# A hybrid encoder on one core: V's turns one a step, projection loads reordered, the time transform's parts alternating, products of zeros ahead of a preparation

## The reference

```
def trunk(x, ...):
    h = rmsnorm(x, attn_norm)
    q, k, v, z = split(h @ attn_w_in, 4)          # 8 heads, two maps of 64 a head, v of 128
    s = q @ k.T * 64 ** -0.5 - slope[head] * abs(t - s)     # for each of the two maps
    p = softmax(s)
    o = (p[:, :, 0] - lam * p[:, :, 1]) @ v
    o = rmsnorm(o, subln_g) * (1 - lam_init)      # over a head's 128
    x = x + (o * silu(z)) @ attn_w_out
    h = rmsnorm(x, fnet_norm)
    u, z = split(h @ fnet_w_in, 2)
    f = real(fft2(u per group of 128, over time and channel))
    x = x + (f * silu(z)) @ fnet_w_out
    return rmsnorm(x, final_norm)
```

## Time and profile before

| | us |
|---|---|
| median of 3 runs | 3275.3 (3273.77 to 3275.41) |
| the profiled execution | 3275.25, span 3273.6 |
| TensorE busy | 2995.3, 91% of the span |
| VectorE, ScalarE, GpSimd busy | 1605.8, 1341.3, 788.7 |
| mean granted TensorE clock | 0.954 of full speed |

### The profile page before, as it was taken

The page is one execution under the profiler, slowest core; times in us unless marked ns, Lnnn a source line. Parts: engine busy times, 40 slices in busy tenths (PEclk is TensorE's granted clock), DMA queues, the critical chain, the costliest instruction groups (busy, mean ns, idle before and its releaser), DMA issues. The chain is left out here.

```text
span 3273.6 us, 42276 instructions
## 1 busy us (share of the span) xinstructions
PE 2995.3 (91%) x15084; PEld 2511.9 (77%) x15084; DVE 1605.8 (49%) x1832; ACT 1341.3 (41%) x2294; POOL 788.7 (24%) x392
## 2 busy tenths in 40 slices
PE   6999999999689999999999999995998898996599
PEld 4888888888568787878787878783677898975487
DVE  7323221111178787878787878784774101431222
ACT  6111100011167776667676767673342322221221
POOL 1223223223022222212121212123331320220552
PEclk9999999999899999999999999997999998898799
DMA  5333332222434313131313131104453513444653
GB/s 171 119 114 113 125 103 67 75 66 67 111 95 151 99 33 99 34 99 33 97 34 93 40 91 41 38 28 160 165 189 114 194 68 105 119 134 144 238 178 109
DMA packets 226332, 340.27 MB, mean 104 GB/s; under 512 B 22315, under 2 KB 172139, under 8 KB 220668
## 3 DMA queue, kind: packets, MB, share of 16 engines
q1 hardware_dynamic: 221548, 321.23, 31.1%
q0 software_dynamic: 4608, 16.78, 1.9%
HBM read 224.68 MB, written 126.03 MB: 107 GB/s over the span
## 5 line engine op out<-in xcount | busy, mean ns | idle before, releaser
L817 DVE TENSOR_REDUCE pa_half_max<-pa_score 128x1 f32<-128x1024 f32 x512 | 625.4, 1222 | 287.7 <-PE pa_score L630 287.7
L760 ACT ACTIVATE pa_p<-pa_score,pa_neg_max 128x1024 f32<-128x1024 f32 x512 | 567.2, 1111 | 74.4 <-DVE pa_neg_max L823 71.1
L894 POOL TENSOR_SCALAR pa_p<-pa_p,pa_inv_sum,pa_lam_neg 128x2048 f32<-128x2048 f32 x128 | 262.6, 2052 | 1072.9 <-DVE pa_inv_sum L844 1072.9
L687 PE MATMUL pa_o_acc<-pa_wt,pa_vv 128*128 128x256 f32 x2048 | 506.6, 381 | 0.1
L626 PE MATMUL pa_score<-pa_ka,pa_qa 128*128 128x512 f32 x1024 | 462.4, 452 | 39.9 <-DMA pa_kb<-const_position 27.0
L118 PE MATMUL ia_acc<-ia_xh,ia_wh 128*128 128x512 f32 (+1 forms) x1280 | 471.8, 369 | 0.0
L119 PE MATMUL ia_acc<-ia_xl,ia_wh 128*128 128x512 f32 (+1 forms) x1280 | 471.7, 368 | 0.0
L120 PE MATMUL ia_acc<-ia_xh,ia_wl 128*128 128x512 f32 (+1 forms) x1280 | 471.4, 368 | 0.0
L630 PE MATMUL pa_score<-pa_kb,pa_qb 96*128 96x512 f32 x1024 | 433.6, 423 | 0.0
L740 ACT ACTIVATE pa_wt<-pa_turned 128x512 f32<-128x512 f32 x512 | 306.0, 598 | 298.6 <-PE pa_turned L658 298.2
L687 PEld LDWEIGHTS pa_o_acc<-pa_wt,pa_vv 128*128 128x128 f32 x2048 | 371.4, 191 | 43.6 <-issue 0.3
(11 more groups left out here) (224 smaller groups left out, 4355.3 us busy)
## 6 DMA issues: line engine op xcount, KB each, us to landing
ia_raw<-attn_w_in POOLq DMA_DIRECT2D x32, 512.0 KB, 5.5
qk_hi<-ia_stage SPq DMA_DIRECT2D x64, 256.0 KB, 2.1
qk_lo<-ia_stage SPq DMA_DIRECT2D x64, 256.0 KB, 2.1
pa_ka<-qk_hi SPq DMA_DIRECT2D x32, 512.0 KB, 6.6
fl_slices<-normed SPq DMA_DIRECT2D x26, 512.0 KB, 6.6
pa_vt<-v SPq DMA_DIRECT2D x8, 1152.0 KB, 5.5
oa_b_in<-o SPq DMA_DIRECT2D x18, 512.0 KB, 4.8
oa_g_in<-attn_gate SPq DMA_DIRECT2D x18, 512.0 KB, 5.9
```

The costliest lines, as they stand in the source:

```text
L687: mm = pe.matmul(o_acc[:], vv[:, k], wt[:, g % 2, k], start=k == 0, stop=k == NB - 1)
L760: act.activation(dst[:, half * HALF:(half + 1) * HALF], score[:, (4 * q + j) % RING].rearrange("p a b -> p (a b)"), ACT.Exp, bias=neg_max[ ...
L817: dve.tensor_reduce(half_max[:, q % 2, n, half:half + 1], score[:, (4 * q + j) % RING].rearrange("p a b -> p (a b)"), AX_X, ALU.max).then_ ...
L894: pool.tensor_scalar(p1[:, par], p1[:, par], inv_sum[:, par, 1:2], lam["neg"][:, 0:1], ALU.mult, ALU.mult).then_inc(p1_scaled, 1)
```

## The change

Four places are changed.

1. In attention one V turn is made in each of the steps 1 to 5, between the third and the fourth quarter of the pair products; ScalarE copies it between its third and fourth exponential. The wait of the second half of a head's first pair for V's last blocks moves to step 5, and V's next load to step 6.
2. In the output projections branch and gate have semaphores of their own, and the row weight has one. Loads, ScalarE's, VectorE's and GpSimd's first operations are put into another order, and in the first projection PE's sums of squares 2 to 5 stand between the products of the first two row tiles.
3. In the Fourier layer the end sums of all even parts are made ahead of the even parts and copied to a tile, and the parts come as even 0, even 1, odd 0, even 2, odd 1, even 3, odd 2, odd 3, on PE and on ScalarE.
4. Ahead of the preparation PE makes 32 products of a tile of zeros, and it waits there only for the channel table; the other two constants are waited for before the time transform.

```diff
@@ attend
-            order += [(t, "v", c) for c in {1: (0, 1), 2: (2,), 3: (3, 4)}.get(t, ())]
+            order += [(t, "v", t - 1)] if 1 <= t <= NC + 1 else []
...
-                    if follows and q == 5:
-                        hold(sp, sp_held, turns, unit(h, 3, "v", 4) + 1)
+                    if follows and q == 6:
+                        hold(sp, sp_held, turns, unit(h, NC + 1, "v", NC) + 1)
                         load_v(h + 1)
...
-                        last = unit(h, 3, "v", NC - 1) if q == 4 else unit(h, q - 1, "w", NC - 1)
-                        pe.wait_ge(turned_out, last + 1)
+                        pe.wait_ge(turned_out, unit(h, q - 1, "w", NC - 1) + 1)
                         wait(pe, o_copied, OUTS * (h - back) + g)
+                    if k0 == 8 and q == 5:
+                        pe.wait_ge(turned_out, unit(h, NC, "v", NC - 1) + 1)
...
                     pair(2)
+                    turn_value(q - 1)
                     pair(3)
-                    for c in range(NC + 1):
-                        turn_value(c)
...
                     exp(2)
+                    if parts["score"] and (q, "v", q - 1) in place:
+                        take_v(h, q, q - 1)
                     exp(3)
-                    for c in range(NC + 1):
-                        if parts["score"] and (q, "v", c) in place:
-                            take_v(h, q, c)
@@ project_rows, SP
-                load_unit(0)
+                load_branch(0)
                 if rms:
-                    sp.dma_start(row_w[:], subln).then_inc(consts_in, 16)
-                load_weight(0)
-                load_weight(1)
-                load_unit(1)
-                if rms:
+                    sp.dma_start(row_w[:], subln).then_inc(row_in, 16)
+                    load_weight(0)
+                    load_branch(1)
+                    load_gate(0)
+                    load_weight(1)
+                    load_gate(1)
+                else:
+                    load_gate(0)
+                    load_weight(0)
+                    load_weight(1)
+                    load_unit(1)
+                for k in range(2, 4):
+                    load_weight(k)
+                if columns is not None:
                     sp.dma_start(ident[:], ident_dram).then_inc(consts_in, 16)
                     sp.dma_start(norm_w[:], column_norm).then_inc(consts_in, 16)
                 if final_norm is not None:
                     sp.dma_start(fn[:], final_norm.to_broadcast([P, D])).then_inc(consts_in, 16)
-                for k in range(2, KB):
+                load_unit(2)
+                for k in range(4, KB):
                     load_weight(k)
-                for n in range(2, 4):
-                    load_unit(n)
+                load_unit(3)
@@ project_rows, GpSimd
-                weight(1)
-                weight(3)
-                for n in range(N_UNITS):
...
-                    if n < 2:
-                        weight(2 * n + 5)
...
+                if rms:
+                    weight(1)
+                    gated_unit(0)
+                else:
+                    gated_unit(0)
+                    weight(1)
+                weight(3)
+                if rms:
+                    weight(5)
+                    gated_unit(1)
+                else:
+                    gated_unit(1)
+                    weight(5)
+                weight(7)
+                for n in range(2, N_UNITS):
+                    gated_unit(n)
@@ project_rows, PE
-                if columns is not None:
-                    pe.wait_ge(consts_in, 16 * n_consts)
...
+                        if rms and k % 2 == 1:
+                            sum_squares(k // 2 + 2)
...
-                    for n in range(3):
-                        sum_squares(n)
+                    sum_squares(0)
+                    sum_squares(1)
                 first_pair(0)
-                if rms:
-                    sum_squares(3)
                 first_pair(1)
-                if rms:
-                    sum_squares(4)
-                    sum_squares(5)
+                if columns is not None:
+                    pe.wait_ge(consts_in, 16 * n_consts)
@@ project_rows, ScalarE, second projection
-                    for k in range(4):
+                    weight(0)
+                    high(0)
+                    for k in range(1, 4):
                         weight(k)
-                    high(0)
+                    high(1)
                     for k in range(4, KB):
                         weight(k)
-                    high(1)
@@ project_rows, VectorE, first projection
                     weight(0)
-                    weight(2)
                     head_inverse(0, 0)
                     head_inverse(0, 1)
                     head_scale(0)
-                    weight(4)
+                    weight(2)
                     head_inverse(1, 0)
                     head_inverse(1, 1)
                     head_scale(1)
+                    weight(4)
                     weight(6)
@@ fourier_layer
+        time_order = [("even", 0), ("even", 1)]
+        for q in range(2, PAIRS):
+            time_order += [("odd", q - 2), ("even", q)]
+        time_order += [("odd", PAIRS - 2), ("odd", PAIRS - 1)]
+        units += [("nyquist",)] + time_order
...
-                pe.wait_ge(consts_in, 64)
...
+                pe.wait_ge(zeroed, 2)
+                for n in range(32):
+                    pe.matmul(ps[:, 7], ac[:, 0, 0, :P], ac[:, 0, 0, :GROUP], start=True, stop=True)
+                pe.wait_ge(consts_in, 32)
                 for g in range(N_PREP):
                     prepare(g)
...
+                pe.wait_ge(ends_in, 32)
...
                 even_transform(PAIRS)
                 for q in range(PAIRS):
-                    even_transform(q)
-                pe.wait_ge(tables_in, 128)
-                pe.wait_ge(out_lo, len(rows_units))
-                for q in range(PAIRS):
-                    odd_transform(q)
+                    mm = end_sum(q)
+                mm.then_inc(ends_summed, 1)
+                for kind, q in time_order:
+                    if (kind, q) == ("odd", 0):
+                        pe.wait_ge(tables_in, 128)
+                        pe.wait_ge(out_lo, len(rows_units))
+                    (even_transform if kind == "even" else odd_transform)(q)
...
+                for kind, q in time_order:
+                    (take_even if kind == "even" else turn_rows)(q)
```

More of the change, by code:

```diff
@@ L1835, in even_transform @@
                             pe.matmul(out[rows, 0], cos_cols(q, 1, 2 * TB)[0:1], extra[0:1], start=False, stop=True)
[L1836 to L1840 removed]
+                        else:
+                            mm = last
+                    if q == PAIRS:
+                        mm = end_sum(q)
                     mm.then_inc(products, 1)
```

89 lines of the change are left out of this document (55 added, 34 removed).

## The result

The changed kernel takes 3168.3 us (median of 4 runs, 3167.35 to 3170.64) where the kernel before takes 3274.6: a ratio of 0.9677, 95% interval 0.9666 to 0.9689, 106 us less. The forecast was 3162. The profiled execution has a span of 3165.3 us instead of 3273.6. Two executions lie far above all others, one of high_free (3419.9 us) and one of the kernel before (6791.5), and are left out of every comparison.

| stage | before | after | gain | forecast |
|---|---|---|---|---|
| attention | 1340.5 | 1283.4 | 57.1 | 57 |
| first output projection | 310.9 | 293.7 | 17.2 | 17 |
| gate projection | 211.7 | 212.0 | -0.2 | 0 |
| Fourier layer, to `nyquist` | 191.0 | 173.4 | 17.6 | 18 |
| Fourier layer, time transform | 89.4 | 82.9 | 6.5 | 9 |

A forecast was written before the change was run, and what follows sets the result against it. PE was busy 91% of the span, so outside its idle 278 us only its waits and low clock could be won. Gains 57 + 17 + 18 + 9 + 12 = 113 us from 3275.3 gave 3162; range 3150 to 3188.

The forecast's parts named there:

- V's turns: Attention: one V turn per step removes PE's waits for V's copies and the low clock behind; gain 57 us, bounds 39 to 64.
- The new wait in front of a V turn: Attention, steps 2, 4 and 5: the V turn after `pair(2)` waits 0.25 us for weight turn 3's copy.
- B: Attention: all 40 V turns wait 0.7 us for the third weight copy; gain only 39, time 3180; chance 0.10.
- C: Attention: V's copy is late for the next step's first turn; at 2.55 us wait plus 1.2 low clock each, 3309; chance 0.03.
- First output projection: Its start: earlier square, reciprocals and gating bring PE's first product 18.8 us earlier; gain 17 us, bounds 10 to 21.
- The first link: First output projection: row weight, with its own semaphore, lands 5.7 us after the stage's first load, letting ScalarE's first square start.
- Preparation: Fourier layer: 32 zeros raise the clock, so the preparation takes 22.4 us instead of 41.0; gain 18 us, bounds -6.4 to 20.
- rival A: Fourier layer: the preparation stays at or falls back to half clock; term +18 becomes about -4, time 3184; chance 0.15.
- Time transform: Fourier layer: odd part 0 two evens earlier brings the high halves' stores forward; gain 9 us, bounds 5 to 12.
- Second output projection: PE starts 18.3 us earlier, then waits 3.6 for GpSimd before the second pair; gain 12 us, bounds 8 to 16.
- The last three terms: Forecast gains of the Fourier layer's preparation, 18 us, its time transform, 9, and the second output projection, 12.
- the sum 113: Whole kernel: the five terms 57 + 17 + 18 + 9 + 12 add, since barriers close the stages; forecast 3162 us.

The follow-up runs named there:

- u_time: Changed kernel with the time transform's parts in the old order, evens then odds, end sums behind each even part: 3175.7 us, ratio 0.9701.
- u_oa: Changed kernel with the first output projection's old orders and waits for all constants, separate semaphores kept, no row-weight wait on ScalarE: 3184.0 us, ratio 0.9726.
- u_zero: Changed kernel without the 32 products of zeros and PE's wait for the zero tile: 3181.1 us, ratio 0.9716.

## The experiments: what the prediction had left uncertain

**Narrow zeros, and fewer** (zeros_narrow, zeros_16).

```diff
-                for n in range(32):
-                    pe.matmul(ps[:, 7], ac[:, 0, 0, :P], ac[:, 0, 0, :GROUP], start=True, stop=True)
+                for n in range(48):
+                    pe.matmul(ps[:, 7, :P + 2], ac[:, 0, 0, :P], ac[:, 0, 0, :P + 2], start=True, stop=True)
```
```diff
-                for n in range(32):
+                for n in range(16):
```

> The changed kernel with 48 products of zeros of 130 columns in place of 32 of 512; at the low clock 48 x 0.215 = 10.3 us, the same length as now. Theory (products as short as the preparation's own keep PE busy but do not raise the clock): the preparation starts where it does now and takes 41 us at 0.50; 18.9 lost and 1 to 2 more, 3168 + 20 = 3188. Rival 1 (it is the unbroken run of products, without the preparation's handovers between groups, that raises it): 22 us at 1.00, 3168. Rival 2 (the clock rises in the course of the preparation): 3175 to 3182.

> The changed kernel with 16 products of zeros in place of 32. In the changed kernel's trace the zeros go at half speed for the first 6 us and the first low part is there 5.5 us after they start. Theory (once the clock has risen nothing more is needed): 16 zeros take some 6.5 us, the preparation starts 3 to 3.6 us earlier and runs at 1.00; 3168 - 3 = 3165. Rival (the clock has not yet risen at their end, or falls at once in the first group): the preparation takes 41 us, 3168 - 3.5 + 20 = 3184.

Measured: narrow 3184.9 us, ratio 0.9728 (0.9712 to 0.9744), the Fourier layer 18.7 us longer; sixteen 3166.1 us, 0.9671 (0.9655 to 0.9687), that stage 3.7 us shorter. The windows of the stage's start and of the preparation, narrow zeros first, then sixteen:

```profile
2676.94:2688.43 11.49, 10.30 (x49) 10.30 (x49) 4.59 (x5) 3.17 (x3) 0.00 (x0) 0.51 0.78 273
2688.43:2729.47 41.04, 41.04 (x193) 40.97 (x193) 15.20 (x26) 13.73 (x27) 2.19 (x1) 0.50 0.26 81
```
```profile
2678.83:2686.30 7.47, 6.29 (x16) 4.97 (x17) 2.68 (x4) 2.12 (x2) 0.00 (x0) 0.55 0.81 283
2686.30:2708.62 22.32, 22.15 (x193) 21.66 (x191) 17.12 (x28) 14.81 (x28) 0.50 (x1) 1.00 0.65 195
```

The same 10 us of zeros, 130 columns wide, leave the clock at 0.50 through the zeros and all of the preparation, 51 us of nearly unbroken work. Behind 6.3 us of zeros 512 columns wide the preparation runs at 1.00 from start to end, PE busy for 22.15 of 22.32 us. With the width another thing changes: weight loads (PEld) are busy for all 10.30 us of the narrow zeros and for 4.97 of 6.29 of the wide ones. No run parts the two, so what about the wide products raised the clock stays open. With sixteen the preparation starts 7.5 us behind the opening, as it does without zeros, so these zeros cost nothing: they fill the time in which VectorE makes the first low part.

**End sums back at each even part's end** (ends_inplace), the parts still alternating.

```diff
-                    if q == PAIRS:
-                        mm = end_sum(q)
+                    if 0 < q < PAIRS:
+                        pe.wait_ge(ends_copied, q)
+                    mm = end_sum(q)
...
+                    act.activation(ends[:, 2 * q:2 * q + 2], ps[:, 6, 2 * q:2 * q + 2], ACT.Copy).then_inc(ends_copied, 1)
```

> The changed kernel, parts alternating, with each even part's ten end-sum products at its own end again and the two end columns copied with the even part. Theory (40 products of 2 columns in a row drop the clock for the first even part): that row's 5.6 us and the 3.7 us of half speed behind it go, 4 x 1.2 us come back inside the even parts; PE is 4.6 us earlier at its last odd part, and the last high store with it: 3168 - 4.5 = 3163.5. Rival 1 (ten such products at a time lower the clock too, at every even part): 3168 or slower. Rival 2 (the high tile's rounds and the stores and not PE set the end): within 1 us of 3168, with gaps ahead of the odd parts' sums on VectorE.

Measured: 3165.9 us, ratio 0.9667 (0.9651 to 0.9683); the Fourier layer is 3.0 us shorter, the first high store comes 5.6 us earlier and the last 3.0. The window from `nyquist` into the last odd part:

```profile
2853.00:2911.80 58.80, 58.80 (x272) 43.58 (x271) 8.13 (x13) 13.66 (x28) 0.00 (x0) 1.00 0.40 150
```

The clock is at 1.00 throughout, so rival 1 is out. On PE the theory was too large: behind the start of `nyquist` its last odd part ends after 60.2 us where it was 63.2, 3.0 earlier and not 4.6, because the half speed behind the row had cost 2.4 us and not 3.7. All 3.0 arrive at the stage's end, so rival 2 is out too. The total alone does not tell this run from no change. Beside u_time, which has the old order with the end sums in the same place, it gives the alternation by itself: the stage is 9.9 us shorter.

**The last high half in a tile of its own** (high_free).

```diff
-        high_tile = results[:, S:2 * S]
+        def high_tile(q):
+            return results[:, S:2 * S] if q < PAIRS - 1 else mix[:].rearrange("p a k t -> p (a k t)")[:, 0:S]
...
-                    wait(act, high_stored, 32 * q)
+                    if q < PAIRS - 1:
+                        wait(act, high_stored, 32 * q)
```

> The changed kernel with the last high half turned into the first half of the tile of even parts, free by then, instead of into the one high tile that the third store still reads. Theory (the last turning waits 6.5 us for the third high store's landing, at 2923.22, though its low half is summed at 2916.7): it is issued 6.5 to 7 us earlier; the three stores now overlap and land more slowly, so 4 to 7 us are left of it, 3161 to 3164. Rival (the stores share a bandwidth that is used up, so that the last byte lands when it did): within 1.5 us of 3168.

Measured: 3167.9 us (three runs, 3167.2 to 3169.0), ratio 0.9674 (0.9654 to 0.9695). SP's queue, the last high store and the next stage's opening:

```profile
2921.47 2.51 SPq L1783 DMA_DIRECT2D f<-fl_mix  x2
2935.53 0.39 SPq L991 DMA_DIRECT2D of_b_in<-f  x1
```

The store is issued 6.5 us earlier (241.4 behind the stage's opening where it was 247.9), and the stage is 0.8 us shorter: from this store to the next opening is 14.1 us where it was 8.4. My theory falls and the rival's time came, but not its reason. These are windows of the changed kernel (its first low half, then its first high half) and of high_free (the last low and the last high half both under way); the last two numbers are the busy share of the DMA engines and GB/s:

```profile
2888.00:2890.00 2.00, 2.00 (x9) 1.63 (x10) 0.00 (x0) 1.15 (x3) 0.00 (x0) 1.00 0.98 401
2891.00:2895.00 4.00, 4.00 (x19) 3.21 (x18) 0.00 (x0) 1.04 (x2) 0.00 (x0) 1.00 0.57 197
```
```profile
2923.00:2931.00 8.00, 0.00 (x0) 0.00 (x0) 0.00 (x0) 0.00 (x0) 0.00 (x0) 0.50 0.58 200
```

A low half, one transfer of 1024 KB, goes at 401 GB/s; a high half, two transfers of 504 KB, goes at 197 with the DMA engines a little over half busy. In high_free the end of the stage goes at that same pace, so the bandwidth is not used up: what lasts is the time that the high halves take at half the low ones' rate. The trace's landings hint at why. A low half lands in sixteen semaphore updates, each of the two transfers of a high half in nine and those of the second after those of the first (2893.24 to 2893.81, then 2895.43 to 2896.84). They have 63 rows each, nine times seven, and 9 of 16 is 0.56, the busy share: as if nine of the sixteen DMA engines did the work. No run stores another number of rows, so this is not shown.

**Weights 5 and 7 on VectorE** (of_dve).

```diff
+                def weight_odd(k):
+                    dve.wait_ge(w_lo_odd, k // 2)
+                    dve.wait_ge(w_hi, k + 1)
+                    dve.tensor_tensor(wl[:, k], raw[:, k % SLOTS], f32(wh[:, k]), ALU.subtract).then_inc(w_lo_odd, 1)
...
                     for k in range(0, KB, 2):
                         weight(k)
+                        if k >= 4:
+                            weight_odd(k + 1)
```

and weights 5 and 7 leave GpSimd's second projection.

> The changed kernel with the low parts of weights 5 and 7 of the second output projection made by VectorE behind its weights 4 and 6 instead of by GpSimd between units 1 and 2. Theory (the second pair of row tiles waits for GpSimd, whose two weights took 6.70 us beside VectorE's 5.99 for two): GpSimd's units 2 and 3 are 6.7 us earlier, PE's 5.6 us wait and the low clock behind it go; 3168 - 8 = 3160. Rival 1 (VectorE's four weights beside GpSimd's gating take 3 us each and come late for the last slabs of the first pair): PE waits 1 to 3 us for of_wl instead, 3163 to 3166. Rival 2 (the pair's wait is made up later in the stage): 3168.

Measured: 3163.6 us, ratio 0.9661 (0.9644 to 0.9678); the stage is 6.2 us shorter. PE at the second pair, then two of VectorE's four weights:

```profile
2974.31 0.50 PE L118 MATMUL of_acc<-of_wh,of_ah 128*128 128x512 f32 x1 [1.61 <-POOL of_al L1081]
```
```profile
2960.51 3.42 DVE L1284 TENSOR_TENSOR of_wl<-of_raw,of_wh 128x1024 fp32r<-128x1024 f32 x1
2963.84 1.21 DVE L1279 TENSOR_TENSOR of_wl<-of_raw,of_wh 128x1024 fp32r<-128x1024 f32 x1
```

The wait is 1.6 us instead of 5.4 and the products behind it run at full speed (0.50, then 0.40 us). One subtraction takes 1.2 us on VectorE while GpSimd is idle (2963.84) and up to 3.4 beside it (2960.51); GpSimd's takes 2.35 alone and 3.4 beside VectorE. That is the size that the forecast had too small. The Trainium skill (GPSIMD Engine Reference, section 1, Specifications) has the two engines share their way to SBUF, with contention when VectorE's instruction has two SBUF inputs; these subtractions have two, and the rows agree.

**V's turn at the step's end** (v_end).

```diff
-                    turn_value(q - 1)
                     pair(3)
+                    turn_value(q - 1)
```

> The changed kernel with V's turn behind the fourth quarter of the pair products, at the step's end, instead of ahead of it; its copy stays between the third and fourth exponential. Theory (where it stands, the turn waits some 0.2 us for weight turn 3's copy in steps 1, 2, 4 and 5, and it gains from 0.4 us more distance): 0.1 to 0.2 us in each of these 32 steps, at most 6 us, 3162 to 3168; step 3, without pair products, stays. Rival (the copy, and the exponential behind it, come 0.4 us later, so that the next step's first turn waits for the one bank): the steps behind a V turn are 0.5 us or more longer, 3180 or more.

Measured: 3161.5 us, ratio 0.9653 (0.9636 to 0.9671); attention takes 1277.5 us, 5.9 less and outside the spread of the others. The interval overlaps the changed kernel's (0.9666 to 0.9689) a little, but the heads tell them apart: from the first V turn to the fifth, heads 2 to 8 take 38.9 us each in the changed kernel and 38.2 or 38.3 here, and the same again in the run of all four edits below. The first head alone is longer, 39.1 instead of 38.6. The five steps of a head are 8.86, 9.66, 8.53, 10.33 and 9.45 us, 46.8 instead of 47.5. The rival's late copy does not show. The two places lie one quarter of the pair products apart, some 0.7 us (1223.44 to 1224.12 in the changed kernel), and that is enough to hide the weight's copy.

**The four that helped, together** (best): sixteen zeros, end sums in place, weights 5 and 7 on VectorE, V's turn at the end.

> Four edits that each made the changed kernel shorter, together: V's turn at the step's end, 16 products of zeros, the end sums at the end of each even part, weights 5 and 7 of the second output projection on VectorE. They lie in different stages or in parts of one that follow each other, so the gains of the profiled stages should add: 6.0 (attention), 3.7 (preparation), 3.0 (time transform), 6.2 (second output projection), 18.9 in all: 3168.3 - 18.9 = 3149.4, range 3146 to 3154. Rival (the preparation's gain only holds where its clock windows fall as they did, or one edit's place in time takes the gain of another): 3155 or more.

Measured: 3150.3 us (5 runs, 3148.5 to 3152.1), ratio 0.9627 (0.9614 to 0.9640), an interval that lies wholly below the changed kernel's 0.9666. Attention takes 1279.6 us (3.8 less), the Fourier layer 249.4 (6.8 less) and the second projection 225.2 (6.3 less). The preparation takes 22.3 us at 1.00. The gains add, within the 3 us to which attention repeats, and the rival is out.

## Why the prediction was right, point by point

**V's turns, 57 forecast, 57.1 measured.** The steps were forecast as 8.86, 10.01, 8.6, 10.01 and 9.74 and are 8.76, 9.93, 8.63, 10.47 and 9.69. The new wait in front of a V turn is 1232.88 - 1231.84 = 1.04 us behind `pair(2)` where 0.86 is the rule without a wait (1223.00 - 1222.14 in step 1): 0.18, forecast 0.25. The step that failed is small: I wrote that behind V's copy stands only the fourth exponential, which PE needs 3 us on. In step 4 the sample's result stands behind it too, and the pair product at 1245.80 needs its bank: 0.3 us of the 0.46 by which step 4 is longer than forecast. The first scores of that step are 0.16 late as well. Rivals B and C did not come: in the steps with pair products the wait is 0.18 and not 0.7, and no step behind a V turn loses over 1 us.

**First output projection, 17 forecast, 17.2 measured.** Every link came within 1.5 us: the square 4.3 us behind the opening (5.7 forecast), reciprocals 10.5 (11.6), PE 25.3 (25.4). The first link is right only in its time: the square no longer waits for the row weight at all. And u_oa shows that 3.9 us come with the semaphores and not with the orders, most of it at unit 2's square, which the prediction did not look at.

**Preparation, 18 forecast, 17.6 measured.** 32 zeros took 10.1 us (8.3 to 10), the clock rose some 6 us into them (3 to 7), the preparation took 22.1 us (22.4). u_zero and zeros_narrow show the cause, and that rival A, staying low, needs only other zeros to come true. The rule of the Trainium skill that the prediction weighed (TensorE: Matmul & The Clock Gate, Part 1, the table of the two states), sustained busy time releases the clock, again disagrees with the rows: 41.08 us without a gap at 0.50 in u_zero.

**Time transform, 9 forecast, 6.5 measured: a term mis-sized.** Behind the start of `nyquist` the four high stores were forecast at 37.0, 48.9, 61.3 and 71.7 us and came at 38.2, 50.3, 62.3 and 74.5. Two terms were too small. The row of 40 end sums took 5.6 us instead of 4.7, and even part 0, at 0.53 of the clock for 6.0 us, lost 2.4: 3.3 together where 2 was assumed. And the last round took 12.2 us where I had taken 10.4 from the earlier trace rows: the third high store, with the fourth low store issued 3.5 us behind it, landed 10 us after its issue. The kernel before had shown that size in its first round, where the low store stands as far behind: 12.1 us from the first to the second high store. high_free shows that the bound of the last store was not as told either. The forecast took the one high tile, free only when its store has landed, for what holds it back; with a tile of its own the last store is issued 6.5 us earlier and the stage ends 0.8 earlier, since its transfer then takes longer.

**Second output projection, 12 forecast, 9.6 measured: a term mis-sized.** PE's first product came 18.4 us earlier (18.3 forecast). The wait ahead of the second pair was 5.4 us instead of 3.6, because GpSimd's two weights took 6.70 and not 4.7: 1.8 of the missing 2.4. PE ran at half speed from 2975.7 to 2981.4 behind it, for which the forecast had allowed 3. of_dve takes both away and gains 6.2.

The last three terms missed by 0.4, 2.5 and 2.4 us, all three too large, and the sum 113 became 108 in the profile and 106 in the medians. The mechanisms of attention, of the preparation and of the second projection's start held, and the first projection's total is right although its parts are not as told.

## What to carry to other kernels

When an operation is slipped into an engine's order, read everything that stands behind it in each kind of step, the rare step too: the cost was in the one step in five where another result shared the queue. A stretch that stays at the low clock in spite of a busy TensorE can be worth more than any wait in the table (19 us here), and it is tested cheaply, by work put into a gap that exists anyway. Before a transfer is moved forward, take from rows how long the transfers from there to the barrier last by themselves: once they fill the time, an earlier issue brings nothing. An experiment that puts an order back can put a wait back with it; read its trace for the wait before the loss is booked to the order.

## What the runs showed of the hardware

- The granted clock is not told by busy time alone: 130-column products back to back stay at 0.50 for 51 us if they start there (zeros_narrow) and at 1.00 for 22 us if they start there (changed kernel).
- 40 products of 2 columns, 5.6 us with PE counted as busy throughout, were followed by 6 us at half speed (changed kernel); ten at a time between wide products were not (ends_inplace).
- A store of 1024 KB in one transfer went at 401 GB/s, one in two transfers of 504 KB (63 rows each) at 197 GB/s with the DMA engines 0.57 busy (changed kernel, 2888 to 2895).
- Elementwise subtractions of 128 x 1024 on VectorE and GpSimd slow each other: 1.2 to 3.4 us and 2.35 to 3.4 us.
